# Openings of three norm blocks formed from x times the root plus y, the reciprocal and the residual rows behind them, and the last norm shared with GpSimd

## The reference, cut to what matters

```python
def rmsnorm(x, g):
    xf = x.astype(F32)
    y = xf * lax.rsqrt(jnp.mean(xf * xf, axis=-1, keepdims=True) + EPS)
    return (y * g.astype(F32)).astype(x.dtype)

# every block, mixer or MLP, in both layers ("sandwich"):
#   xn = rmsnorm(x, g_pre);  y = block(xn);  x = x + rmsnorm(y, g_post)
# layer 0: mixer AB (projection IN_AB, recurrence and attention, projection OUT_AB), MLP (UP0, DOWN0)
# layer 1: mLSTM (IN_C, convolutions, chunked recurrence, OUT_C), MLP (UP1, DOWN1)
# MLP: relu(xn @ up) ** 2 @ down
```

## Time and profile before

| what | value |
|---|---|
| timed runs | 1105.33, 1105.84, 1106.32 us (median 1105.84) |
| profiled execution, first to last instruction (span) | 1106.5 us |
| granted TensorE clock over the span | 0.990 |
| PE busy | 1053.1 us, 95% |
| DVE busy | 653.9 us, 59% |
| ACT busy | 530.0 us, 48% |
| POOL busy | 184.5 us, 17% |

### The profile page before, as it was taken

The page is one execution under the profiler, slowest core; times in us unless marked ns, Lnnn a source line. Parts: engine busy times, 40 slices in busy tenths (PEclk is TensorE's granted clock), DMA queues, the critical chain, the costliest instruction groups (busy, mean ns, idle before and its releaser), DMA issues.

```text
span 1106.5 us, 21578 instructions
## 1 busy us (share of the span) xinstructions
PE 1053.1 (95%) x8479; PEld 913.2 (83%) x8479; DVE 653.9 (59%) x960; ACT 530.0 (48%) x862; POOL 184.5 (17%) x250
## 2 busy tenths in 40 slices
PE   5999999899999999999899999899989999999995
PEld 5988778689999999998899945363529999999995
DVE  5567694643475543336996566767784485544333
ACT  5333654543566553435565344462624557553431
POOL 5134000000114220101400430412100104220100
PEclk9999999999999999999999999999989999999998
DMA  9799898999435445443743069999998435445431
GB/s 352 256 339 348 316 332 287 389 376 405 156 134 172 163 161 171 169 158 128 276 140 129 1 202 407 350 403 348 388 393 316 164 123 169 159 167 171 163 122 43
DMA packets 92762, 261.23 MB, mean 236 GB/s; under 512 B 8933, under 2 KB 10085, under 8 KB 92409
## 3 DMA queue, kind: packets, MB, share of 16 engines
q1 hardware_dynamic: 91818, 258.69, 65.0%
q0 software_dynamic: 432, 1.29, 0.4%
q10 hardware_dynamic: 432, 0.14, 0.1%
HBM read 218.36 MB, written 41.73 MB: 235 GB/s over the span
## 4 chain that ended last, share of the span: by engine, by line
PE 80%; DVE 10%; ACT 4%; issue 2%; POOL 2%; DMA 1%; SPq 1%; DVEq 0%; ACTq 0%
PE ps L2096 20%; PE ps L2097 20%; PE ps L2098 20%; PE ps L2208 2%; PE ps L2610 2%; PE ps L2571 2%; PE ps L2596 1%; PE ps L2289 1%; DVE cring L1787 1%; PE ps L2463 1%; DVE w_lo L1243 1%; PE ps L2190 1%; DMA w_raw<-in_weights 1%; DVE x L1328 1%; PE ps L2451 1%
## 5 line engine op out<-in xcount | busy, mean ns | idle before, releaser
L1243 DVE TENSOR_TENSOR w_lo<-w_raw,w_hi 128x1024 fp32r<-128x1024 f32 x232 | 286.5, 1241 | 209.8 <-ACT w_hi L718 209.1
L718 ACT ACTIVATE w_hi<-w_raw 128x1024 fp32r<-128x1024 f32 x232 | 242.4, 1054 | 209.9 <-PE ps L2098 173.2
L2096 PE MATMUL ps<-xin_hi,w_hi 128*128 128x288 f32 x1016 | 304.6, 300 | 14.8 <-DVE w_lo L1243 14.8
L2097 PE MATMUL ps<-xin_lo,w_hi 128*128 128x288 f32 x1016 | 301.5, 297 | 0.0
L2098 PE MATMUL ps<-xin_hi,w_lo 128*128 128x288 f32 x1016 | 301.2, 296 | 0.0
L2096 PEld LDWEIGHTS ps<-xin_hi,w_hi 128*128 128x128 f32 x1016 | 192.8, 190 | 26.6 <-DVE w_lo L1243 16.2
L2097 PEld LDWEIGHTS ps<-xin_lo,w_hi 128*128 128x128 f32 x1016 | 192.7, 190 | 0.7
L2098 PEld LDWEIGHTS ps<-xin_hi,w_lo 128*128 128x128 f32 x1016 | 192.6, 190 | 0.0
L2097 PE MATMUL ps<-hid_lo,w_hi 128*128 128x288 f32 x512 | 151.0, 295 | 0.0
L2098 PE MATMUL ps<-hid_hi,w_lo 128*128 128x288 f32 x512 | 150.9, 295 | 0.0
L2096 PE MATMUL ps<-hid_hi,w_hi 128*128 128x288 f32 x512 | 150.2, 293 | 0.0
(11 more groups left out here) (414 smaller groups left out, 1657.0 us busy)
## 6 DMA issues: line engine op xcount, KB each, us to landing
w_raw<-in_weights SPq DMA_DIRECT2D x232, 512.0 KB, 3.3
...
```

The lines of the kernel that those rows point to most:

```text
L718: act.activation(w_hi[:, l % UM], w_raw[:, l % W_SLOTS], ACT.Copy).then_inc(hi_ready, 1)
L1243: dve.tensor_tensor(w_lo[:, l % W_SLOTS], w_raw[:, l % W_SLOTS], w_hi[:, l % UM], ALU.subtract).then_inc(lo_ready, 1)
L2096: pe.matmul(out, w_hi[:, j, ws], hi, start=start and kk == 0, stop=False)
L2097: pe.matmul(out, w_hi[:, j, ws], lo, start=False, stop=False)
```

## The change

A norm cancels a factor common to a column, so an input norm may read x times such a factor. The changed kernel opens the next projection with `xs = x * std + y`, which is the new x times `std`, and so needs no reciprocal ahead of it. The small constant in the next norm is kept right by adding `EPS * std * std` to the sum of squares. Part by part:

- DVE's `residual` waits for `std` and multiplies the first three pieces of x by it; POOL (`scaled_rows`) multiplies the last two, of 2 tiles and 1 tile. DVE does all five additions.
- Behind the opening DVE forms the constant's term and adds it, and takes the reciprocal `rinv`, which lies in the part of `par` that is no longer used; this stands between `w_lo` of steps 4 and 5.
- POOL forms the real new x, tile by tile, `y * rinv` and `x + y` (`new_rows`): in UP0 and UP1 one tile ahead of each of the first eight pairs of `hid_lo`, in IN_C all eight in a row ahead of the folds for the gates.
- PE's second group of unread matmuls is 7 instead of 12, and waits for `std`.
- The last norm: DVE does 6 tiles in three pieces, POOL the last 2 (`last_rows`).

```diff
-GAP = 12
+GAPS = (12, 7)
...
+OF_DVE = 3
+LAST_PIECES = [(0, 2), (2, 4), (4, 6)]
...
+        xs, o = at("xs", behind_xm, MT, T)
+        x2, o = at("x2", o, MT, T)
+        rinv = par[:, AT["conv_a_w"]:AT["conv_a_w"] + T]
...
-            sp.wait_ge(x_new, 2 * MT)
+            sp.wait_ge(xs_ready, 2 * MT)
...
+                if m + 2 < MT:
+                    sp.wait_ge(x_new, 3 * MT + m + 2)
+                else:
+                    sp.wait_ge(xs_scaled, 2 * 3 + 1)
...
 
             sp.wait_ge(kv_stored, 32)
@@ -744,18 +756,23 @@
                 act.wait_ge(mean_ready, s + 1)
                 if s >= 1:
                     act.wait_ge(rstd_ready, s)
-                act.activation(std, ps[:, 7, 0:T], ACT.Sqrt, bias=tiny[:, 0:1], scale=1.0 / D).then_inc(std_ready, 1)
+                if s % 2 == 0 and s:
+                    act.activation(std, ps[:, 7, 0:T], ACT.Sqrt, scale=1.0 / D).then_inc(std_ready, 1)
+                else:
+                    act.activation(std, ps[:, 7, 0:T], ACT.Sqrt, bias=tiny[:, 0:1], scale=1.0 / D
+                                   ).then_inc(std_ready, 1)
 
             def norm_in(s, n, gain, layer, between=None, ph=None):
 
                 if ph:
                     act_hi(OPEN, 0, STEP0[ph])
+                if n == 1:
+                    act.wait_ge(kv_stored, 32)
                 for m in range(MT):
-                    if n:
-                        act.wait_ge(x_new, MT * (n - 1) + m + 1)
-                    act.activation(xin_hi[:, m], x[:, m], ACT.Copy, scale=pcol(gain, layer * MT + m)
+                    act.wait_ge(xs_ready, MT * (n - 1) + m + 1)
+                    act.activation(xin_hi[:, m], xs[:, m], ACT.Copy, scale=pcol(gain, layer * MT + m)
                                    ).then_inc(xin_hi_ready, 1)
-                    act.activation(y[:, m], x[:, m], ACT.Square).then_inc(sq_ready, 1)
+                    act.activation(x2[:, m], xs[:, m], ACT.Square).then_inc(sq_ready, 1)
                 if between:
                     between()
                 for g in range(OPEN + 1, BEHIND if ph else 0):
@@ -774,6 +791,8 @@
                     m = l if ph == OUT_AB else it * UM + j
                     act.wait_ge(step_done, STEP0[ph] + 8 * groups * it + l + 1)
                     act.wait_ge(sq_added, ADDED[s] + m - 1)
+                    if s > 1:
+                        act.wait_ge(x_new, MT * (s // 2))
                     out = ps[:, out_bank(ph, l), 0:T]
                     act.activation(sq[:, j % 2], out, ACT.Square).then_inc(sq_ready, 1)
                     act.activation(y[:, m], out, ACT.Copy, scale=pcol(gain, layer * MT + m)
...
-                        dve.wait_ge(x_new, MT * (n - 1) + m + 1)
-                    dve.scalar_tensor_tensor(xin_lo[:, m], x[:, m], pcol(gain, layer * MT + m), xin_hi[:, m],
-                                             ALU.mult, ALU.subtract).then_inc(xin_ready, 1)
+                        dve.wait_ge(xs_ready, MT * (n - 1) + m + 1)
+                    dve.scalar_tensor_tensor(xin_lo[:, m], (xs if new else x)[:, m], pcol(gain, layer * MT + m),
+                                             xin_hi[:, m], ALU.mult, ALU.subtract).then_inc(xin_ready, 1)
...
-                    order.after(dve.tensor_tensor(y[:, 0:4], y[:, 0:4], y[:, 4:8], ALU.add))
-                    order.after(dve.tensor_tensor(y[:, 0:2], y[:, 0:2], y[:, 2:4], ALU.add))
-                    dve.tensor_tensor(sqsum, y[:, 0], y[:, 1], ALU.add).then_inc(sq_added, 1)
+                    order.mark(dve.scalar_tensor_tensor(rinv, std, EPS * D / P, std, ALU.mult, ALU.mult))
+                    order.after(dve.tensor_tensor(x2[:, 0:4], x2[:, 0:4], x2[:, 4:8], ALU.add))
+                    order.after(dve.tensor_tensor(x2[:, 0:2], x2[:, 0:2], x2[:, 2:4], ALU.add))
+                    order.after(dve.tensor_tensor(x2[:, 0], x2[:, 0], rinv, ALU.add))
+                    dve.tensor_tensor(sqsum, x2[:, 0], x2[:, 1], ALU.add).then_inc(sq_added, 1)
+                    dve.reciprocal(rinv, std).then_inc(rstd_ready, 1)
                     dve_lo(OPEN + 2, 0, STEP0[ph])
                     dve_lo(OPEN + 3, 0, STEP0[ph])
...
             def residual(s):
 
-                stat_rstd(s)
+                n = s // 2
+                if n:
+                    dve.wait_ge(x_new, MT * n)
+                else:
+                    dve.wait_ge(kv_stored, 32)
+                dve.wait_ge(std_ready, s + 1)
 
                 def scale(i):
                     a, b = PIECES[i]
-                    order.mark(dve.tensor_tensor(y[:, a:b], y[:, a:b], rstd.unsqueeze(1).to_broadcast([P, b - a, T]),
-                                                 ALU.mult))
+                    if i < OF_DVE:
+                        order.mark(dve.tensor_tensor(xs[:, a:b], x[:, a:b], std.unsqueeze(1).to_broadcast([P, b - a, T]),
+                                                     ALU.mult))
 
                 def add(i):
                     a, b = PIECES[i]
-                    order.wait()
+                    if i < OF_DVE:
+                        order.wait()
+                    else:
+                        dve.wait_ge(xs_scaled, 2 * n + i - OF_DVE + 1)
+                    dve.tensor_tensor(xs[:, a:b], xs[:, a:b], y[:, a:b], ALU.add).then_inc(xs_ready, b - a)
+                return scale, add
+
+            def last_rows():
+
+                stat_rstd(7)
+                dve.wait_ge(x_new, 3 * MT)
+                for a, b in LAST_PIECES:
+                    order.after(dve.tensor_tensor(y[:, a:b], y[:, a:b], rstd.unsqueeze(1).to_broadcast([P, b - a, T]),
+                                                  ALU.mult))
                     dve.tensor_tensor(x[:, a:b], x[:, a:b], y[:, a:b], ALU.add).then_inc(x_new, b - a)
-                return scale, add
...
-            scale, add = residual(7)
-            for i in range(len(PIECES)):
-                scale(i)
-                add(i)
+            last_rows()
...
+            def scaled_rows(s):
+
+                n = s // 2
+                if n:
+                    pool.wait_ge(x_new, MT * n)
+                else:
+                    pool.wait_ge(kv_stored, 32)
+                pool.wait_ge(std_ready, s + 1)
+                for a, b in PIECES[OF_DVE:]:
+                    pool.tensor_tensor(xs[:, a:b], x[:, a:b], std.unsqueeze(1).to_broadcast([P, b - a, T]), ALU.mult
+                                       ).then_inc(xs_scaled, 1)
+
+            def new_rows(s, m):
+
+                pool.wait_ge(rstd_ready, s + 1)
+                order.after(pool.tensor_tensor(y[:, m], y[:, m], rinv, ALU.mult))
+                pool.tensor_tensor(x[:, m], x[:, m], y[:, m], ALU.add).then_inc(x_new, 1)
+
+            def last_rows():
+
+                a, b = LAST_PIECES[-1][1], MT
+                pool.wait_ge(x_new, 3 * MT)
+                pool.wait_ge(rstd_ready, 8)
+                order.after(pool.tensor_tensor(y[:, a:b], y[:, a:b], rstd.unsqueeze(1).to_broadcast([P, b - a, T]),
+                                               ALU.mult))
+                pool.tensor_tensor(x[:, a:b], x[:, a:b], y[:, a:b], ALU.add).then_inc(xs_scaled, 1)
...
-                with pool.Fori(0, 16) as it:
+                for it in range(MT):
+                    new_rows(s, it)
+                    body(it)
+                with pool.Fori(MT, 16) as it:
                     body(it)
...
-            hidden_low(0)
+            scaled_rows(1)
+            hidden_low(0, 1)
             square_sums(3)
+            scaled_rows(3)
...
+            for m in range(MT):
+                new_rows(3, m)
...
-            hidden_low(1)
+            scaled_rows(5)
+            hidden_low(1, 5)
             square_sums(7)
+            last_rows()
...
-                unread(base, GAP)
-                pe.wait_ge(rstd_ready, 2 * n)
-                unread(base, GAP)
+                unread(base, GAPS[0])
+                pe.wait_ge(std_ready, 2 * n)
+                unread(base, GAPS[1])
```

8 lines of the change are left out of this document (6 added, 2 removed).

## The result

The changed kernel took 1126.26 us, median of four runs (1124.76 to 1126.63), beside 1106.08 us (1105.33 to 1107.56) for the kernel before on the same chip: a ratio of 1.0175, 95% interval 1.0161 to 1.0189. It is 20 us slower. The forecast of 1120.6 had the sign and most of the mechanism, and was 5.7 us short; the time lies in the range of 1108 to 1128, at its upper edge, and 0.3 us above the forecast's own range of 1115 to 1126.

The account below looks back on a forecast made before the run. The prediction took PE, with 80% of the chain, as the bound; UP0 +3.1, IN_C +7.9, UP1 +3.1 and the end +0.7 sum to +14.8 us on 1105.84, about 1120.6 us, range 1108 to 1128 (8 in 10).

Parts of the forecast that it names:

- Openings, turns: Start of UP0, IN_C, UP1: POOL and DVE alternate, blocking each other, so the saved reciprocal leaves −0.27, +0.10, −0.27 us.
- Openings, clock: Start of UP0, IN_C, UP1: PE's longer idle stretch lowers its clock, 1.7 us a fall; part of rival 2.
- rival 2: Longer PE idle in openings lowers its clock, 1.7 us per fall, three openings and one in IN_C: 1127 us; chance 0.12.
- Step 5: In UP0, IN_C and UP1, DVE's added work behind the opening delays `w_lo`; PE stops for 1.27 us.
- Steps 7 and 11: UP0 and UP1: PE stops 0.8 us at step 7 (late reciprocal and `relu`), 1.3 at step 11 (POOL's added operations).
- IN_C: Turns with POOL's rows and folds plus DVE's late start delay step 12's `w_lo`; PE loses 7.9 us, step 5 included.
- IN_C, clock: In IN_C's projection, behind the opening: one more fall of PE's clock, costing 1.7 us; part of rival 2.
- Rival 1: IN_C absorbs the turns and costs about 2.2 us: total +9, 1115 us; chance 0.18.
- The end: Last norm: DVE takes two turns with POOL, and SP issues two stores, 0.34 us apart, instead of one: +0.7 us.
- Rivals 3: In openings POOL and DVE run side by side, keeping the 1.99 us gain: total −3.5, 1102 us; chance 0.14.
- 4 (nothing is seen): Turns in the openings, but losses behind them covered: 1106 us; chance 0.06.

Follow-up runs that it names:

- open_dve: Changed kernel with VectorE doing all five pieces of the opening's row multiplications, GpSimd none: 1119.47 us.
- more_unread: Changed kernel with PE's second group of unread matmuls 22 instead of 7: 1124.32 us.
- recip_behind: Changed kernel with the reciprocal `rinv` moved from ahead of `w_lo` of steps 5 and 6 to behind them, in all three openings: 1127.18 us.
- rows_in_down: Changed kernel with GpSimd forming the residual rows of UP0 and UP1 behind all of `hid_lo`, in DOWN0 and DOWN1: 1123.08 us.
- narrow_folds_first: Changed kernel with IN_C's row operations 8 columns wide instead of 288 and moved behind the gate folds: 1117.80 us.
- last_dve: Changed kernel with only the last norm as before, VectorE alone in five pieces: 1122.88 us.

## Why the forecast was right, and where it was short

- *Openings, turns* (−0.27, and +0.10 in IN_C): right, −0.23 and +0.03. The first add took 1.58 us (1.5 foretold), and by open_dve the turns are what eats the reciprocal.
- *Openings, clock* (rival 2, chance 0.12, left out of the sum): this is the term that failed. I had PE's idle stretch right (2.1 foretold, 1.96 measured), and the row of a fall behind a stretch of 1.77, and still gave the fall little weight because the other stretch of 1.79 brought none. The clock fell behind all three openings in the changed kernel's trace; more_unread gives 0.9, 1.0 and 1.3 us for them, less than the 1.7 of the rival. (I take it that the rows come slower than a fast PE would take them: 16 matmuls in the window of more_unread, 13 at the lower clock, where the rival had 33 against 19.) That is more than all of what was short in UP0 and UP1, 0.74 and 1.07 us.
- *Step 5* (+1.27): right as a stop, 1.15. It was no independent term: taking the reciprocal out from there only moved the stop to step 7 (recip_behind). What I overlooked is DVE's idle time ahead of `w_lo` of step 4, where 2.3 of the 2.80 us would have cost nothing in UP.
- *Steps 7 and 11* (+0.8, +1.3): over-sized, 0.55 and 0.71. Together with what follows from them, the rows in UP cost 1.6 us (rows_in_down).
- *IN_C* (+7.9): measured 7.87, and that it is so close is luck. `w_lo` of step 12 was to be 9.6 to 11 us late and was 8.9, of which 1.0 is the opening's fall of the clock, which was not in the sum: the turns and the late start alone brought 7.9, and the forecast had them at least 1.7 too high. `hs` was 7.4 late, and the last 0.5 came far behind the projection. That it is turns of rows and of folds, and not DVE's late start, is shown by narrow_folds_first. Rival 1, that IN_C absorbs the turns, is excluded by the 7.4 us and by the mean of 696 ns for a convolution operation.
- *IN_C, clock*: rival 2 had one more fall there, and it came, at 0.50 behind the stop of 3.08 us. It cost nothing that can be seen. last_dve and rows_in_down have the same stop (3.09 and 3.08 us) and matmuls at 240 ns for 2.6 and 2.9 us behind it instead of 5.8, and `hs` comes no sooner in them (+7.7 and +7.9): PE at full clock only waits longer for DVE at step 12 (1.19 and 1.20 us instead of 0.59).
- *The end* (+0.7): +1.30. The last add was 0.1 later than foretold; the rest is the stores, 0.8 us longer, which I had at 0.34.
- Rivals 3 (engines don't meet) and 4 (nothing is seen) fell: the first add took 1.58 us, and every stage behind an opening became longer.
- Of the 3.4 us between the 14.8 of the sum and the 18.2 of the spans, 1.8 lie in UP0 and UP1 (the clock there is 2.1), 0.6 at the end, and 1.0 ahead of UP0, which is scatter. The other 2.0 us of the medians' difference come from the long profiled execution of the kernel before, as said above.
